# A linear-attention scan: scratch laid out by chunk, two states of a head stacked on the partitions

## The reference, cut to what matters

```python
def gla_scan(q, k, v, g, strict):
    ...
    def step(state, inp):
        qc, kc, vc, gc = inp
        b = jnp.cumsum(gc, axis=2)
        ...
        o = jnp.einsum('bhij,bhjv->bhiv', att, vc) + jnp.einsum('bhid,bhdv->bhiv', qc * jnp.exp(b), state)
        b_last = b[:, :, -1, :]
        state = jnp.exp(b_last)[..., None] * state + jnp.einsum(
            'bhjd,bhjv->bhdv', kc * jnp.exp(b_last[:, :, None, :] - b), vc)
        return state, o
    ...
    o_f = gla_scan(q, k, v, g_f, False)
    o_b = flip(gla_scan(flip(q), flip(k), flip(v), flip(g_b), True))
    o = rms_norm((o_f + o_b).astype(z.dtype), g_norm).reshape(B, S, GLA_WIDTH)
    return o * jax.nn.silu(z)
```

## Time and profile before

| what | us |
|---|---|
| median of 3 runs (lowest, highest) | 2980.94 (2978.84, 2982.73) |
| the profiled execution | 2989.56 |
| its span, first to last instruction | 2987.8 |
| TensorE busy in it | 2878.2 (96%) |
| VectorE, ScalarE, GpSimd busy | 1611.9, 1363.7, 1141.9 |

### The profile page before, as it was taken

The page is one execution under the profiler, slowest core; times in us unless marked ns, Lnnn a source line. Parts: engine busy times, 40 slices in busy tenths (PEclk is TensorE's granted clock), DMA queues, the critical chain, the costliest instruction groups (busy, mean ns, idle before and its releaser), DMA issues.

```text
span 2987.8 us, 48655 instructions
## 1 busy us (share of the span) xinstructions
PE 2878.2 (96%) x15972; PEld 2394.4 (80%) x15972; DVE 1611.9 (54%) x2749; ACT 1363.7 (46%) x2458; POOL 1141.9 (38%) x1118
## 2 busy tenths in 40 slices
PE   4999999988999999999999999999999999999998
PEld 4768888777788888887887888878887888888887
DVE  6567777766677777774335222255557555532111
ACT  4652254566455555553236111256556656532111
POOL 0211111245233333332330763177676767623221
PEclk8999999989999999999999999999999999999999
DMA  7243355487211111112652332342335332244231
GB/s 266 72 125 104 104 161 163 160 280 234 71 59 58 56 57 56 56 56 90 212 186 102 140 146 84 102 134 95 102 103 183 105 102 95 93 166 158 94 103 56
DMA packets 285737, 357.65 MB, mean 120 GB/s; under 512 B 20196, under 2 KB 190308, under 8 KB 285063
## 3 DMA queue, kind: packets, MB, share of 16 engines
q1 hardware_dynamic: 282536, 344.43, 35.3%
q0 software_dynamic: 3072, 11.54, 0.9%
HBM read 241.99 MB, written 113.90 MB: 119 GB/s over the span
## 4 chain that ended last, share of the span: by engine, by line
PE 84%; DVE 4%; issue 4%; ACT 4%; DMA 2%; POOL 2%; SPq 0%; DVEq 0%; ACTq 0%; POOLq 0%
PE PS L2999 6%; PE PS L3007 6%; PE PS L3003 6%; PE PS L2358 4%; PE PS L2359 4%; PE PS L2360 4%; PE PS L342 4%; PE PS L344 4%; PE PS L343 4%; PE PS L1779 4%; PE PS L1757 4%; PE PS L2526 4%; PE PS L2527 3%; PE PS L2528 3%; PE PS L1780 2%
## 5 line engine op out<-in xcount | busy, mean ns | idle before, releaser
L342 PE MATMUL PS<-hTh,whi 128*128 128x512 f32 x640 | 257.9, 403 | 1.5 <-DVE hTl L296 1.1
L2999 PE MATMUL PS<-hTh,wc 128*128 128x512 f32 x896 | 243.6, 394 | 8.9 <-DVE zu L2933 6.1
L344 PE MATMUL PS<-hTh,wlo 128*128 128x512 f32 x640 | 250.6, 392 | 0.0
L343 PE MATMUL PS<-hTl,whi 128*128 128x512 f32 x640 | 250.3, 391 | 0.0
L2755 POOL TENSOR_TENSOR wc<-wpr,wc 128x512 fp32r<-128x512 f32 x128 | 176.3, 1377 | 181.4 <-ACT wc L2751 181.4
L1860 ACT ACTIVATE pb__164<-PS,nm,rq 128x512 f32<-128x512 f32 x256 | 197.1, 779 | 101.7 <-DVE nm L1923 101.4
L3003 PE MATMUL PS<-hTh,wc 128*128 128x512 f32 x896 | 240.5, 390 | 0.0
L3007 PE MATMUL PS<-hTl,wc 128*128 128x512 f32 x896 | 239.9, 390 | 0.2 <-DVE hTl L2699 0.2
L2358 PE MATMUL PS<-ow_h,of_h 128*128 128x512 f32 x576 | 224.2, 389 | 1.4 <-DVE oy L2309 1.4
L2360 PE MATMUL PS<-ow_h,of_l 128*128 128x512 f32 x576 | 224.1, 389 | 0.0
L2359 PE MATMUL PS<-ow_l,of_h 128*128 128x512 f32 x576 | 224.1, 389 | 0.0
(11 more groups left out here) (303 smaller groups left out, 7113.7 us busy)
## 6 DMA issues: line engine op xcount, KB each, us to landing
wpr<-wuz SPq DMA_DIRECT2D x128, 256.0 KB, 3.4
projT<-pev SPq DMA_DIRECT2D x80, 256.0 KB, 2.7
xt<-x SPq DMA_DIRECT2D x8, 2048.0 KB, 8.1
mw<-wmod SPq DMA_DIRECT2D x64, 256.0 KB, 2.8
oxt<-x SPq DMA_DIRECT2D x32, 512.0 KB, 4.6
sg_v<-vev SPq DMA_DIRECT2D x64, 256.0 KB, 2.4
...
```

What stands on the lines that cost most here:

```text
L342: pe.matmul(PS[:, bank, :], w[1][:, s, k, :], hTh[:, k, b], start=(k == 0), stop=False)
L343: pe.matmul(PS[:, bank, :], w[1][:, s, k, :], hTl[:, k, b], start=False, stop=False)
L344: mm = pe.matmul(PS[:, bank, :], w[2][:, s, k, :], hTh[:, k, b], start=False, stop=(k == KD - 1))
L2999: pe.matmul(o, wc[:, k, 0, kk, :], h_tile(hTh, k, kk), start=(kk == 0 and not onto), stop=False, skip_group_check=onto)
```

## The change

- The scratch `cumT` goes; `chnk[16 chunks, 128 partitions, 16 slots, 128 tokens]` holds, for a chunk and partition, four slots of decay sums, four of keys and queries, four of values, four of the gate. `proj_store` and `gates_store` write a block of 512 tokens of such a tile in four pieces of 512 bytes a partition (48 of the 80 blocks, and all 16 of the sums). The other tiles stay in `projT`.
- `main_fk` reads sums, keys and queries of a chunk with one DMA (4 KB a partition) into `m_in`. The loads of `m_z` and the backward scan's loads of values and decays read one run a partition; `level_fe` and `level_kq` change likewise.
- The forward and backward state of a head lie on the two halves of the partitions of one tile `m_sc` (three buffers): the forward state of a head on its own 64, the backward one of the same head on the other 64. `main_vs` loads values alone; `main_states` loads the backward state in two DMAs of 64 partitions, crossing the halves. In the loop it comes behind `load(t + 4)`, for chunk t + 3, with a wait for `s_mo`.
- `q_states` writes a head's queries times forward decay on its own half and times backward decay on the other, in four instructions; `qf` has no zeros any more, and GpSimd's two memsets go. `state` has four instructions of 64 partitions instead of two of 128. `outputs` has two products for a head instead of three, and waits for the loaded states.
- Before the loop VectorE clears two halves of `m_sc` and copies the last backward state into the other two.
- The stores of the latent queries (`nope_store`, `rope_store`, the latter with each half written twice) stay as they were, on SyncE.

```diff
+
+
+C_CUM, C_KQ, C_V, C_Z = 0, 4, 8, 12
+C_SLOT = {**{T_GK + n: C_KQ + n for n in range(4)}, **{T_GV + n: C_V + n for n in range(4)},
+          **{T_GZ + n: C_Z + n for n in range(4)}}
...
-    cumT = scratch("cumT", (4, P, S))
+    chnk = scratch("chnk", (NT, P, 16, P))
...
         def proj_store(sp, j):
...
-            sp.dma_start(projT[g, :, tb * 512:(tb + 1) * 512], pev[:, j % 2, :]).then_inc(s_pst[j % 2], 16)
+            if g in C_SLOT:
+                dst = chnk[4 * tb:4 * tb + 4, :, C_SLOT[g], :].rearrange("t p c -> p t c")
+                sp.dma_start(dst, pev[:, j % 2, :].rearrange("p (t c) -> p t c", t=4)).then_inc(s_pst[j % 2], 16)
+            else:
+                sp.dma_start(projT[g, :, tb * 512:(tb + 1) * 512], pev[:, j % 2, :]).then_inc(s_pst[j % 2], 16)
...
-                sp.dma_start(cumT[n, :, tb * 512:(tb + 1) * 512], gcum[:, u, :]).then_inc(s_gst, 16)
+                sp.dma_start(chnk[4 * tb:4 * tb + 4, :, C_CUM + n, :].rearrange("t p c -> p t c"),
+                             gcum[:, u, :].rearrange("p (t c) -> p t c", t=4)).then_inc(s_gst, 16)
...
         def level_fe(sp, t, p):
-            s, tok = t % 2 * 2 + p, slice(t * P, (t + 1) * P)
+            s = t % 2 * 2 + p
...
-            sp.dma_start(l_fe[:, o:o + 2 * P].rearrange("p (d c) -> p d c", d=2), cumT[p:4:2, :, tok].rearrange("d p c -> p d c")
+            sp.dma_start(l_fe[:, o:o + 2 * P].rearrange("p (d c) -> p d c", d=2), chnk[t, :, C_CUM + p:C_CUM + 4:2, :]
...
-            sp.dma_start(l_fe[:, o + 2 * P:o + 3 * P], cumT[p, :, tok]).then_inc(s_ll[s], 16)
+            sp.dma_start(l_fe[:, o + 2 * P:o + 3 * P], chnk[t, :, C_CUM + p, :]).then_inc(s_ll[s], 16)
...
         def level_kq(sp, t, p):
-            s, tok = t % 2 * 2 + p, slice(t * P, (t + 1) * P)
+            s = t % 2 * 2 + p
...
-            sp.dma_start(l_kq[:, s, :, :], projT[T_GK + 2 * p:T_GK + 2 * p + 2, :, tok].rearrange("d p c -> p d c")
-                         ).then_inc(s_lk[s], 16)
+            sp.dma_start(l_kq[:, s, :, :], chnk[t, :, C_KQ + 2 * p:C_KQ + 2 * p + 2, :]).then_inc(s_lk[s], 16)
...
-            sp.dma_start(kt[:, :, :], projT[T_GK:T_GK + 4:2, :, back_tok(n)].rearrange("h p c -> p h c")).then_inc(s_bl[0], 16)
-            sp.dma_start(vt[:, :, :], projT[T_GV:T_GV + 4, :, back_tok(n)].rearrange("h p c -> p h c")).then_inc(s_bl[0], 16)
+            sp.dma_start(kt[:, :, :], chnk[NT - 1 - n, :, C_KQ:C_KQ + 4:2, :]).then_inc(s_bl[0], 16)
+            sp.dma_start(vt[:, :, :], chnk[NT - 1 - n, :, C_V:C_V + 4, :]).then_inc(s_bl[0], 16)
...
         def back_decay(sp, n):
...
-            sp.dma_start(et[:, :, :], cumT[2:4, :, back_tok(n)].rearrange("h p c -> p h c")).then_inc(s_bl[1], 16)
+            sp.dma_start(et[:, :, :], chnk[NT - 1 - n, :, C_CUM + 2:C_CUM + 4, :]).then_inc(s_bl[1], 16)
...
-            pool.wait_ge(s_pb, 8 + NBLK - 2)
-            for p in range(2):
-                pool.memset(qf[p][:, :, :, :], 0.0).then_inc(s_gm, 1)
...
-        m_fe = [at("m_fe%d" % s, M0 + 8 * s * K, [P, 2, 2, P]) for s in range(4)]
-        m_kq = [at("m_kq%d" % s, M0 + (8 * s + 2) * K, [P, 2, 2, P]) for s in range(4)]
+        m_in = [at("m_in%d" % s, M0 + 8 * s * K, [P, 2, 2, 2, P]) for s in range(4)]
+        m_fe = [m_in[s][:, 0] for s in range(4)]
+        m_kq = [m_in[s][:, 1] for s in range(4)]
...
-        m_vs = [at("m_vs%d" % s, M0 + (32 + 8 * s) * K, [P, GH * DV + 2 * DV]) for s in range(4)]
+        m_vs = [at("m_vs%d" % s, M0 + (32 + 8 * s) * K, [P, GH * DV]) for s in range(4)]
...
-        m_st = at("m_st", M0 + 30 * K, [P, 2, 2, DV])
+        m_sc = [at("m_sc%d" % j, M0 + o * K, [P, 2, 2, DV]) for j, o in enumerate((30, 66, 74))]
...
-        qf = [at("qf%d" % p, M0 + (64 + 8 * p) * K, [P, 2, GH, P]) for p in range(2)]
+        qf = [at("qf%d" % p, M0 + (64 + 8 * p) * K, [P, 2, 2, P]) for p in range(2)]
...
         def main_fk(sp, t):
-            s, tok = t % 4, slice(t * P, (t + 1) * P)
-            sp.dma_start(m_fe[s].rearrange("p d h c -> p (d h) c"), cumT[0:4, :, tok].rearrange("n p c -> p n c")
-                         ).then_inc(s_ml[s], 16)
-            sp.dma_start(m_kq[s].rearrange("p h w c -> p (h w) c"), projT[T_GK:T_GK + 4, :, tok].rearrange("n p c -> p n c")
-                         ).then_inc(s_ml[s], 16)
+            sp.dma_start(m_in[t % 4].rearrange("p a b d c -> p (a b d) c"), chnk[t, :, C_CUM:C_V, :]).then_inc(s_ml[t % 4], 16)
...
         def main_vs(sp, t):
...
+            sp.dma_start(m_vs[t % 4][:, :], gla_vs[t, :, 0:GH * DV]).then_inc(s_mla[t % 4], 16)
+
+        def main_states(sp, t):
...
-            sp.dma_start(m_vs[t % 4][:, :], gla_vs[t, :, :]).then_inc(s_mla[t % 4], 16)
+            for e in range(2):
+                sp.dma_start(m_sc[t % 3][HALF[1 - e], e].rearrange("p h v -> p (h v)"), gla_vs[t, HALF[e], GH * DV:]
+                             ).then_inc(s_msl[t % 3], 16)
...
         def main_factors(act, t):
...
-            act.wait_ge(s_ml[s], 32 * (t // 4 + 1))
+            act.wait_ge(s_ml[s], 16 * (t // 4 + 1))
...
-                act.wait_ge(s_mqf, 2 * (t - 1))
+                act.wait_ge(s_mqf, 4 * (t - 1))
...
+                if t + 3 < NT:
+                    sp.wait_ge(s_mo, t + 1)
+                    main_states(sp, t + 3)
...
         def main_dve(dve):
...
-            dve.memset(m_st[:, 0, :, :], 0.0).then_inc(s_gm, 1)
+            dve.wait_ge(s_bs, 2 * NT)
+            for e in range(2):
+                dve.memset(m_sc[0][HALF[e], e], 0.0).then_inc(s_gm, 1)
+                dve.tensor_copy(m_sc[0][HALF[1 - e], e], st[HALF[e], (NT - 1) % 2, :, :]).then_inc(s_gm, 1)
...
-            dve.wait_ge(s_gm, 8)
+            dve.wait_ge(s_gm, 9)
...
-                    r = slice(DK * e, DK * e + DK)
-                    dve.tensor_tensor(qf[t % 2][r, :, e:GH:2, :],
-                                      m_kq[s][r, :, 1].unsqueeze(1).broadcast_to([DK, 2, 2, P]),
-                                      m_x[t % 2][r, 0:2], ALU.mult).then_inc(s_mqf, 1)
+                    r, q = HALF[e], HALF[1 - e]
+                    dve.tensor_tensor(qf[t % 2][r, e], m_kq[s][r, :, 1], m_x[t % 2][r, 0], ALU.mult).then_inc(s_mqf, 1)
+                    dve.tensor_tensor(qf[t % 2][q, e], m_kq[s][r, :, 1], m_x[t % 2][r, 1], ALU.mult).then_inc(s_mqf, 1)
...
             def state(t):
...
-                    dve.wait_ge(s_ms, 2 * t)
+                    dve.wait_ge(s_ms, 4 * t)
...
-                    dve.scalar_tensor_tensor(m_st[:, 1 - t % 2, p, :], m_st[:, t % 2, p, :], gtot[:, p, t:t + 1],
-                                             PS[:, 7, p * DV:(p + 1) * DV], ALU.mult, ALU.add).then_inc(s_ms, 1)
+                    for e in range(2):
+                        r = HALF[e]
+                        dve.scalar_tensor_tensor(m_sc[(t + 1) % 3][r, e, p, :], m_sc[t % 3][r, e, p, :], gtot[r, p, t:t + 1],
+                                                 PS[r, 7, p * DV:(p + 1) * DV], ALU.mult, ALU.add).then_inc(s_ms, 1)
...
             def outputs(t):
...
-                pe.wait_ge(s_mqf, 2 * t + 2)
+                pe.wait_ge(s_mqf, 4 * t + 4)
...
-                    pe.wait_ge(s_ms, 2 * t)
+                    pe.wait_ge(s_ms, 4 * t)
+                    pe.wait_ge(s_msl[t % 3], E_msl[t % 3] + 32 * ((t + 2) // 3))
...
-                    pe.wait_ge(s_gm, 8)
+                    pe.wait_ge(s_gm, 9)
...
-                    back = m_vs[s][:, (GH + h // 2) * DV:(GH + 1 + h // 2) * DV] if t else st[:, (NT - 1) % 2, h // 2, :]
...
-                    pe.matmul(o, qf[t % 2][:, 0, h, :], m_st[:, t % 2, h // 2, :], start=False, stop=False)
-                    mm = pe.matmul(o, qf[t % 2][:, 1, h, :], back, start=False, stop=True)
+                    mm = pe.matmul(o, qf[t % 2][:, h % 2, h // 2, :], m_sc[t % 3][:, h % 2, h // 2, :], start=False, stop=True)
```

More of the change, by code:

```diff
@@ L468, in emit @@
         gtots = at("gtots", X0 + 69 * K + 320, [P, 4, NT])
+        HALF = (slice(0, DK), slice(DK, P))
         ga = at("ga", X0 + 24 * K, [2 * RANK, S])
@@ L721, in emit @@
         s_bss = [sem("s_bss0"), sem("s_bss1")]
-        def back_tok(n):
-            return slice((NT - 1 - n) * P, (NT - n) * P)
         def back_load(sp, n):
@@ L849, in proj_sp @@
                     main_vs(sp, 1)
+                    main_states(sp, 1)
                 if n == -1:
@@ L1035, in emit @@
         s_ml = [sem("s_ml%d" % s) for s in range(4)]
+        s_msl, E_msl = (s_gtot, s_const, s_set), (2 * NG + 1, 48, 4)
         s_msx = sem("s_msx")
@@ L1388, in load_z @@
                     sp.wait_ge(s_mgz, t - 3)
-                sp.dma_start(m_z[t % 4][:, :, :], projT[T_GZ:T_GZ + 4, :, t * P:(t + 1) * P].rearrange("h p c -> p h c")
-                             ).then_inc(s_mzl[t % 4], 16)
+                sp.dma_start(m_z[t % 4][:, :, :], chnk[t, :, C_Z:C_Z + 4, :]).then_inc(s_mzl[t % 4], 16)
             def store(t):
@@ L1401, in main_sp @@
             load(2)
+            main_states(sp, 2)
             level_store(sp, NU - 1)
```

(6 more changed lines are left out.)

2 lines of the change are left out of this document (1 added, 1 removed).

## The result

The changed kernel takes 2996.39 us (median of 6 runs, 2995.58 to 2999.70) against 2981.84 for the kernel before in the same comparison (2978.84 to 2991.10). The ratio is 1.0037, with a 95% interval of 1.0023 to 1.0050: slower by 11 us (7 to 15), outside the range that was forecast. The profiled execution takes 2999.7 us.

What follows compares the result with a forecast made beforehand. TensorE was taken to bound one scan step of four, VectorE one, queues and short chains the rest. -5.7 + 2.6 + 0.3 + 0.2 + 1.2 = -1.4 us gave 2979.5 us, range 2975 to 2985.

Steps and rivals of the forecast that it cites:

- Part 1: Scan outputs on TensorE: two products a head instead of three, 1.2 us in steps 1, 5, 9, 13, 0.9 in 15; -5.7 us.
- Part 2, the price on VectorE: Scan, VectorE's split instructions: state +0.52 us, query products +0.06, with a contended one 0.1 more; +0.65 us a chunk.
- Part 2, the place: VectorE's +0.65 us lies on the path in steps 3, 7, 11 before `rsw` and 14 at `ck`; +2.6 us.
- step 4k+3: Third scan step of each four: VectorE full from query products through state to `rsw`, TensorE waiting 3.02 us, 3.84 in step 3.
- step 4k+2: Second scan step of each four: SyncE reaches the store of `nst` 6.7 us after the outputs; its landing releases ScalarE.
- Part 5, the clock: Longer TensorE waits for `rsw` in steps 7 and 11 lower its clock behind them; +1.2 us, bounds 0 and 2.5.
- Start: Ahead of the loop: VectorE's two memsets and two copies for one memset, against earlier chunk 0 outputs; +0.3 us.
- Parts 3 and 4: SyncE and DMA queue in the scan, +0.2 us in steps 6 and 10; 512-byte stores of the projections, cost 0.
- VectorE is the bound: Rival, chance 0.17: VectorE's 0.65 us counts in 15 chunks, with low TensorE clock after waits; 2992 at most, about 2988 otherwise.

Runs made afterwards that it cites:

- twoprod: Kernel before with the product of queries and backward state left out of the outputs, two products a head instead of three: 2979.5 us, ratio 0.9978.
- state4: Kernel before with VectorE's two state instructions split into four of 64 partitions, upper and lower half in turn: 2995.6 us, ratio 1.0029.
- q4: Kernel before with VectorE's two query products of 64x512 a chunk split into four of 64x256, not crossing halves: 2986.9 us, ratio 1.0009.
- layout: Kernel before with only the chunk-by-chunk scratch, its 512-byte stores and one load for decay sums, keys and queries: 2983.7 us, ratio 0.9994.
- state4h: Kernel before with the two state instructions split into four of 64 partitions, grouped by half: 2988.2 us, ratio 1.0010.

## Why the prediction was wrong, point by point

- **Part 1, TensorE: right in size.** -5.7 forecast, -6.6 measured by twoprod. Eight pairs take 1.78 us. The steps that were to give it (1, 5, 9 and 13) do not show it one by one.
- **Part 2, the price on VectorE: the step that failed first.** It took each further instruction at the 0.26 by which two neighbours start apart. Halves in turn do not start before the last has finished: the state costs +0.88, not +0.52. The query products were +0.06 to +0.13. They are +0.36 undisturbed (1.77 against 1.41), +1.40 in steps 6 and 10, and +0.36 to +0.68 in the others, with GpSimd at work. The row that said so was there: 1.82 instead of 1.41 for two is one stop of 0.4, and four instructions can be stopped up to four times. The Trainium skill states it ("SBUF — State Buffer", SBUF: two separate sides): a VectorE instruction with two SBUF inputs and a GpSimd one that reads SBUF exclude each other for the whole instruction. The ends at the same 0.28 us behind GpSimd's agree. But a product takes 0.42 alone, so not all of it waits. That was read from traces, no run took GpSimd's work away.
- **Part 2, the place: the step that failed most.** The sum let VectorE count in step 4k+3, before `rsw`, and saw SyncE and the `nst` store in step 4k+2. In the steps 4k+3 `rsw` came no later: the product behind it starts 10.8, 10.6 and 10.6 us into steps 3, 7 and 11, before 10.9, 10.5 and 11.0. The 0.65 us put there three times are not there. In step 4k+2 `ck` stands behind the same products and state, and TensorE already waited 0.83 us for it. Add the parts: 0.83, +0.89 for outputs that end four pairs sooner (worked out from the earlier trace rows; in twoprod, where TensorE also stops ahead of the weighted keys, 0.58 of it shows in this wait), +1.01 for the state (state4 waits 1.84), +1.39 for the query products (q4 waits 2.22): 4.12. Measured: 4.07.
- **Part 5, the clock: right in kind, too small.** Before, TensorE ran at its lower level behind one wait for `ck` or `rsw` (3.84 us, step 3) and at full clock behind the two of 3.02 and 3.03. After, it ran low behind six: `rsw` in steps 3, 7 and 11 (4.44, 4.90, 4.02) and `ck` in steps 6, 10 and 14 (4.07, 4.07, 3.04). Each costs 1.5 us (3.56 against 2.06). Half of 2.5 us was put in, and it is five times 1.5. The lengths of the waits alone do not tell: 3.02 us in step 11 of layout had the low clock behind it, and 3.88 in step 7 of state4h did not.
- **Start: +2.35 us in step 0**, and +3.0 in steps 0 to 2 together, not +0.3. Two memsets and two copies were counted. What was not is that two groups of query products and the first state follow them in line on VectorE, which is 1.2 us later by the memsets and copies, 0.6 by the products and 0.9 by the state. TensorE's second contribution waits 2.5 us for that `m_sc`.
- **Parts 3 and 4: right** for the stores in 512-byte pieces (projections busy 260 of 260 us, layout alone 0.9994). In layout the packets of the scan fell from 44,685 to 25,758 for the same bytes, and ScalarE's wait for the `nst` store from 17.1 to 15.2 us, with no gain in time. The two rates of the earlier trace rows, 341 and 419 GB/s, are of different traffic, so their difference need not be the price of packet size. The half loads are settled only to within 0.3 to 6.6 us. Nobody waited for one.

By steps, the 15.0 us by which attention begins later are: steps 0 to 2 +3.0; steps 6, 10 and 14 +10.9 (`ck` later 6.15, low clock 4.76); steps 3, 7 and 11 +2.3; 4, 8 and 12 -2.4; 5, 9 and 13 +1.95; behind the start of step 15 -0.75.

The rival that came true is "VectorE is the bound", and its mechanism came near: it has VectorE's longer work and the clock, but spreads them over 15 chunks, where three steps 4k+2 have 10.9 of the 15.0 us. Its price was the same 0.65 us, its time 2992 at most, and its chance of 0.17 was kept low by "VectorE is idle 55 of these 170 us". That is an average over the steps, and its engine stands full just where `ck` is awaited.
